# Griffin-style decoder step on one Trainium2 core: the attention scores of a tile's two heads issued alternately

## The chip, the cores and the metric

The kernel runs on one core of a Trainium2 chip. The metric is the device time of one execution in microseconds (us), taken as the median of several runs. Engines are named as in the profile: PE is TensorE's matmul side, PEld its weight loads, DVE is VectorE, ACT is ScalarE, POOL is GpSimd, SP is SyncE (which only issues transfers here).

## The reference, cut to what matters

One layer of a hybrid decoder is applied to a prompt of 1024 tokens and to 8 single new tokens. A recurrent branch (RG-LRU) and an attention branch are merged by gates and followed by a SwiGLU FFN. The change touches the prompt's attention alone. It has three groups of eight heads, each head 64 wide, with (window, dilation) of (128, 1), (512, 4) and (2048, 16). For each head the computation is

```python
s = jnp.einsum('brcqhe,brckhe->brchqk', qb, kb) * (HEAD_DIM ** -0.5)
s = jnp.where(valid[:, None], s + bias, -jnp.inf)
m = jnp.max(s, axis=-1)
p = jnp.exp(s - m[..., None])
l = jnp.sum(p, axis=-1)
o = jnp.einsum('brchqk,brckhe->brcqhe', p, vb.astype(jnp.float32))
```

where a block of 128 queries sees one or two blocks of 128 keys of its own residue class.

## The kernel before, in words

All activations lie transposed, channels on the 128 partitions and the 1032 tokens along the free dimension. Most of the time goes to large projections: weights are split into a high and a low part, and three matmuls of 344 columns per weight tile are summed (line 456, in the function `unit`).

The prompt's attention is a stage of its own (`for g in range(NG)`, line 543 and on for PE). It has three groups g, and for each a loop of four iterations i, twelve iterations in all. One iteration handles one tile of 128 channels, which holds two heads: head 0 on partitions 0 to 63, head 1 on partitions 64 to 127. The tile's queries QT, keys KTT and values VT are loaded by SP, with the bias tables BT of the two heads.

Each iteration has 8 steps, n = 0 to 7. A step is one head hh and one pair of query blocks bp (two blocks of 128 tokens). In the kernel before the order is head, then block pair: `hh, bp = n // 4, n % 4`. A step passes through these operations:

- **scores** on PE, line 576: two matmuls (m = 0, 1) with the head's 64 rows; the result is 128 x 128 or 128 x 256 and goes to the PSUM bank `s_bank[n % 2]`. As data are fp32, each of these matmuls runs as two passes, and each pass is a weight load followed by a MATMUL row in the trace. So a step has four passes of scores.
- scale and bias on DVE (line 1209), row maximum (line 1215), its negative (line 1217); then the exponential on ACT (line 957), in the tile `SB[n % 2]`.
- **turns** on PE, line 587: two to four 128 x 128 transposes of the probabilities with all 128 rows, evacuated by ACT (lines 948 and 950) into `PTS`.
- **values** on PE, line 599: probabilities times values, 128 rows, evacuated by DVE (line 1223).

PE works on three steps at once. Its loop over n runs from 0 to 9, and in turn n it issues the scores of step n, the turns of step n - 1, the values of step n - 2, and then some **pieces** of an unrelated projection (line 556), which keep it busy while DVE and ACT work. The list PIECES sets how many: 7, 5, 4, 4, 4, 4, 3, 3, 3 and 3 pieces of three matmuls in the turns 0 to 9, and 8 pieces stand ahead of turn 0.

```python
PIECES = (8, 15, 20, 24, 28, 32, 36, 39, 42, 45, 48)
...
s_bank = [ups[:, 1, 0, :], ups[:, 1, 1, :]]
pt_bank = [ups[:, 1, 2, :], aux[:, 0, :]]
```

The order is written out by hand and held together by semaphores. For this change these count: `s_mm` (scores of a step are in PSUM, DVE waits for it), `sa_done` (DVE has read a bank of scores, PE waits for it before it writes the bank again, and SP waits for all eight before it loads the next tile), `exp_done` (PE's turns wait for it) and `pt_ev` (values wait for it). For group 0 the tokens of a block lie side by side in QT and KTT; in groups 1 and 2 they are every fourth or every eighth token (the function `toks`), so PE reads them with a stride. The function `nkeys` says how many key blocks a query block sees: in group 0 two, except for the first block; in group 1 alternately one and two; in group 2 one.

Of the kernel before, what the change touches and what calls it, by code (L numbers as in the profile page):

```python
# [28 lines left out]
P = 128  # L29
# [7 lines left out]
HD = 64  # L37
# [55 lines left out]
def build(nc, A, O):  # L93

    with ExitStack() as ctx:
# [174 lines left out]
        def nkeys(g, b):  # L270

            return (2 if b else 1, 1 + b % 2, 1)[g]
# [172 lines left out]
        def _(pe):  # L445
# [100 lines left out]
            for g in range(NG):  # L546
                with pe.Fori(0, 4) as i:
                    def pieces(a, b):
                        for n in range(a, b):
                            slot, c, k = n // 24, n // 8 % 3, n % 8  # L550
                            if n % 24 == 0:
                                pe.wait_ge(w_split[slot], i + (T0[f"att{g}"] + 2))
                            if n % 8 == 0:
                                pe.wait_ge(au_ev, i * 6 + (24 * g + n // 8 + 1))
                            for w, a2 in ((0, 0), (0, 1), (1, 0)):
                                ins = nc.tensor.matmul(ups[:, 0, c, 0:CH], wsp[:, slot, w, k, :], big1[:, a2, k, c * CH:(c + 1) * CH],  # L556
                                                       start=(k == 0 and w + a2 == 0), stop=(k == KT - 1 and w == 1))
                            if n % 8 == 7:
                                ins.then_inc(au_mm if c < NCH - 1 else unit_done[slot], 1)

                    pieces(0, 8)
                    pe.wait_ge(v_ld, i * 16 + 16 * (4 * g + 1))
                    pe.wait_ge(pt_ev, i * 8 + (32 * g + 2))
                    for b in range(8):
                        ins = nc.tensor.transpose(pt_bank[b // 4][:, (b % 4) * P:(b % 4 + 1) * P], toks(VT, g, b), ident[:])
                    ins.then_inc(vt_mm, 1)
                    pe.wait_ge(qk_ld, i * 48 + 48 * (4 * g + 1))
                    for n in range(10):
                        if n < 8:
                            hh, bp = n // 4, n % 4  # L570
                            hr = slice(hh * HD, (hh + 1) * HD)
                            pe.wait_ge(sa_done, i * 8 + (32 * g + n + 1))
                            for m in range(2):
                                b = 2 * bp + m
                                nk = nkeys(g, b)
                                ins = nc.tensor.matmul(s_bank[n % 2][:, 256 * m + 256 - P * nk:256 * m + 256], toks(QT, g, b)[hr],  # L576
                                                       toks(KTT, g, b, nk)[hr], start=True, stop=True)
                            ins.then_inc(s_mm, 1)
                        if 1 <= n <= 8:
                            q = n - 1  # L580
                            pe.wait_ge(exp_done, i * 8 + (32 * g + q + 1))
                            pe.wait_ge(pt_ev, i * 8 + (32 * g + q + 1))
                            if q == 0:
                                pe.wait_ge(vt_ev, i + (4 * g + 1))
                            for m in range(2):
                                for c in range(256 * m + 256 - P * nkeys(g, 2 * (q % 4) + m), 256 * m + 256, P):
                                    ins = nc.tensor.transpose(pt_bank[q % 2][:, c:c + P], SB[q % 2][:, c:c + P], ident[:])  # L587
                            ins.then_inc(pt_mm, 1)
                        if n >= 2:
                            q = n - 2  # L590
                            hh, bp = q // 4, q % 4
                            pe.wait_ge(pt_ev, i * 8 + (32 * g + q + 3))
                            pe.wait_ge(o_ev, i * 8 + (32 * g + q + 1))
                            for m in range(2):
                                b = 2 * bp + m
                                nk = nkeys(g, b)
                                for k in range(nk):
                                    c = 256 * m + 256 - P * (nk - k)
                                    ins = nc.tensor.matmul(o_bank[:, m * (HD + 1):(m + 1) * (HD + 1)], PTS[q % 2][:, c:c + P],  # L599
                                                           VTOK[:, b + 1 - nk + k, hh, :], start=(k == 0), stop=(k == nk - 1))  # L600
                            ins.then_inc(pv_mm, 1)
                        pieces(*PIECES[n:n + 2])
# [132 lines left out]
        def _(act):  # L735
# [149 lines left out]
            for n in range(4):  # L885
                i, j = n // 2, n % 2
# [21 lines left out]
            for g in range(NG):  # L908
                with act.Fori(0, 4) as i:
# [31 lines left out]
                    for n in range(9):  # L941
                        if n >= 1:
                            q = n - 1
                            act.wait_ge(pt_mm, i * 8 + (32 * g + q + 3))
                            act.wait_ge(pv_mm, i * 8 + (32 * g + q + 1))
                            lo = 256 - P * nkeys(g, 2 * (q % 4))
                            if g < 2:
                                ins = nc.scalar.activation(PTS[q % 2][:, lo:512], pt_bank[q % 2][:, lo:512], ACT.Copy)
                            else:
                                ins = nc.scalar.activation(PTS[q % 2].rearrange("p (m c) -> p m c", m=2)[:, :, P:2 * P],  # L950
                                                           pt_bank[q % 2].rearrange("p (m c) -> p m c", m=2)[:, :, P:2 * P], ACT.Copy)
                            ins.then_inc(pt_ev, 1)
                        if n < 8:
                            act.wait_ge(nm_done, i * 8 + (32 * g + n + 1))
                            for m in range(2):
                                cols = slice(256 * m + 256 - P * nkeys(g, 2 * (n % 4) + m), 256 * m + 256)
                                ins = nc.scalar.activation(SB[n % 2][:, cols], SB[n % 2][:, cols], ACT.Exp,  # L957
                                                           bias=NM[:, 2 * (n % 2) + m:2 * (n % 2) + m + 1])
                            ins.then_inc(exp_done, 1)
                        if n in (0, 2, 4, 6, 8):  # L960
                            evac(n // 2)
# [78 lines left out]
        def _(dve):  # L1040
# [154 lines left out]
            for g in range(NG):  # L1195
                per = 2 if g == 1 else 1
                with dve.Fori(0, 4) as i:
# [2 lines left out]
                    step.loop(i, 8)  # L1200
                    for n in range(10):
                        if n < 8:
                            hh, bp = n // 4, n % 4
                            dve.wait_ge(s_mm, i * 8 + (32 * g + n + 1))
                            dve.wait_ge(pt_mm, i * 8 + (32 * g + n + 1))
                            for m in range(2):
                                nk = nkeys(g, 2 * bp + m)
                                cols = slice(256 * m + 256 - P * nk, 256 * m + 256)
                                ins = nc.vector.scalar_tensor_tensor(SB[n % 2][:, cols], s_bank[n % 2][:, cols], SCALE,  # L1209
                                                                     BT[:, hh, 0:P * nk][:, ::-1], ALU.mult, ALU.add)  # L1210
                            ins.then_inc(sa_done, 1)
                            dve.wait_ge(sa_done, i * 8 + (32 * g + n + 3))
                            for m in range(2):
                                cols = slice(256 * m + 256 - P * nkeys(g, 2 * bp + m), 256 * m + 256)
                                ins = nc.vector.tensor_reduce(OT[:, 2 * bp + m, hh, HD + 1:HD + 2], SB[n % 2][:, cols], AX_X, ALU.max)  # L1215
                            step.step(ins)
                            ins = nc.vector.tensor_scalar(NM[:, 2 * (n % 2):2 * (n % 2) + 2], OT[:, 2 * bp:2 * bp + 2, hh, HD + 1],  # L1217
                                                          -1.0, None, ALU.mult).then_inc(nm_done, 1)
                        if n >= 2:
                            q = n - 2  # L1220
                            hh, bp = q // 4, q % 4
                            dve.wait_ge(pv_mm, i * 8 + (32 * g + q + 3))
                            ins = nc.vector.tensor_copy(OT[:, 2 * bp:2 * bp + 2, hh, 0:HD + 1],  # L1223
                                                        o_bank[:, 0:2 * (HD + 1)].rearrange("p (m e) -> p m e", m=2)).then_inc(o_ev, 1)
# [249 lines left out]
```

## Time and profile before

| what | value |
|---|---|
| median of 3 runs | 2247.6 us (2247.16 to 2249.08) |
| profiled execution | span 2250.2 us; no other time is listed for it |
| PE busy | 2160.0 us, 96% of the span |
| PEld busy | 2059.9 us, 92% |
| DVE, ACT, POOL busy | 39%, 23%, 25% |
| share of the final chain on PE | 90% |
| of it line 456, 556, 576 | 62%, 12%, 6% |

Lines 576 (scores), 587 (turns), 599 (values) and 556 (pieces) occur only in the attention stage. A PE row's duration is the time one matmul was under way; neighbours overlap, so what a matmul costs is read from the distance between starts, or from the chain, which gives each piece the time for which it alone held up the end.

### The profile page before, as it was taken

How to read it: one execution, taken by the hardware profiler on the slowest of the kernel's cores; microseconds unless marked ns; L12 is line 12 of the kernel's file. 1: busy time of each engine (PE TensorE's matmuls, PEld its weight loads, DVE VectorE, ACT ScalarE, POOL GpSimd, SP SyncE). 2: the span in 40 equal slices, each digit the busy share in tenths (PEclk: the TensorE clock that was granted, in tenths of full speed). 3: DMA queues.
4: the chain of work that ended last, by engine and by line, in shares of the span. 5: the costliest groups of instructions: out<-in, count | busy, mean ns of one | idle time of the engine just before them, and what ended most of it. 6: DMA issues, size and time to landing. Idle time of an engine off the chain costs nothing.

```text
span 2250.2 us, 33517 instructions
## 1 busy us (share of the span) xinstructions
PE 2160.0 (96%) x13052; PEld 2059.9 (92%) x13052; DVE 877.7 (39%) x1212; ACT 510.9 (23%) x796; POOL 556.6 (25%) x337
## 2 busy tenths in 40 slices
PE   5799899999899999999989999989999999999999
PEld 4799799999888888889989999979999999999999
DVE  8466667777223322232343444261221122211211
ACT  4466533333133332333310001031000000000000
POOL 3232232232311111111111123323333322233322
PEclk9899899999999999999997789989999999999999
DMA  3111022222432233224255334211111111111112
GB/s 123 40 40 48 29 79 75 93 82 86 151 132 89 89 113 117 80 89 139 81 207 222 104 132 149 88 35 47 47 37 47 47 47 47 47 47 47 47 45 87
DMA packets 71402, 188.39 MB, mean 84 GB/s; under 512 B 9257, under 2 KB 28668, under 8 KB 70652
## 3 DMA queue, kind: packets, MB, share of 16 engines
q1 hardware_dynamic: 41392, 136.97, 18.2%
q10 hardware_dynamic: 29964, 50.78, 6.2%
q8 instruction: 31, 0.51, 0.1%
q14 instruction: 15, 0.12, 0.0%
HBM read 145.06 MB, written 45.81 MB: 85 GB/s over the span
## 4 chain that ended last, share of the span: by engine, by line
PE 90%; DVE 5%; issue 1%; ACT 1%; DMA 1%; ACTq 0%; POOL 0%; SPq 0%; DVEq 0%; POOLq 0%
PE ups L456 62%; PE ups L556 12%; PE ups L576 6%; PE aux L599 3%; PE aux L643 1%; PE aux L480 1%; PE aux L621 1%; DVE ext L1066 1%; PE aux L507 1%; PE ups L587 1%; PE aux L587 1%; DVE ext L1062 1%; DVE big L1057 1%; DVE big_f L1051 0%; DVE big L1401 0%
## 5 line engine op out<-in xcount | busy, mean ns | idle before, releaser
L456 PE MATMUL ups<-big,wsp 128*128 128x344 f32 x9360 | 1528.3, 325 | 31.0 <-DVE big L1057 8.2
L456 PEld LDWEIGHTS ups<-big,wsp 128*128 128x128 f32 x9360 | 1501.9, 191 | 54.5 <-issue 26.4
L424 POOL CAST wsp<-wraw 128x1024 fp32r<-128x1024 f32 (+2 forms) x160 | 164.1, 1026 | 1611.6 <-issue 749.6
L426 POOL TENSOR_TENSOR wsp<-wraw,wsp 128x1024 fp32r<-128x1024 f32 (+2 forms) x160 | 380.6, 2379 | 12.8
L556 PE MATMUL ups<-big,wsp 128*128 128x344 f32 x1728 | 304.6, 328 | 6.9 <-ACTq L904 6.9
L556 PEld LDWEIGHTS ups<-big,wsp 128*128 128x128 f32 x1728 | 273.2, 190 | 12.2 <-ACTq L904 7.2
L1162 DVE RECIPROCAL x<-x 128x1024 f32<-128x1024 f32 x24 | 157.3, 6554 | 75.1 <-ACT x L864 75.1
L1209 DVE SCALAR_TENSOR_TENSOR x<-ups,ext 128x128 f32<-128x128 f32 (+1 forms) x192 | 58.7, 348 | 311.9 <-PE ups L576 230.7
L1398 DVE TENSOR_TENSOR ext<-ext,ups 128x1032 f32<-128x1032 f32 x22 | 27.0, 1229 | 373.3 <-PE ups L456 373.3
L576 PE MATMUL ups<-x 64*128 64x128 f32 (+1 forms) x384 | 132.3, 473 | 2.8 <-DMA ext<-bt_s 2.8
L1025 ACT ACTIVATE ext<-ups 128x1032 f32<-128x1032 f32 x22 | 22.7, 1031 | 489.9 <-PE ups L456 489.8
L1410 DVE TENSOR_TENSOR x<-ups,x 128x1032 f32 x24 | 29.6, 1233 | 217.9 <-PE ups L456 217.9
L576 PEld LDWEIGHTS ups<-x 64*128 64x128 f32 x384 | 85.4, 279 | 23.7 <-issue 21.4
L957 ACT ACTIVATE x<-x,ext 128x128 f32<-128x128 f32 (+1 forms) x192 | 76.2, 444 | 82.5 <-DVE ext L1217 82.5
L599 PE MATMUL aux<-ext,x 128*128 128x65 f32 x560 | 73.2, 266 | 0.0
L599 PEld LDWEIGHTS aux<-ext,x 128*128 128x128 f32 x560 | 70.6, 192 | 0.0
L1401 DVE CAST big<-ext 128x1032 f32 x22 | 56.8, 2582 | 7.4 <-DVE ext L1398 7.4
L1215 DVE TENSOR_REDUCE x<-x 128x1 f32<-128x128 f32 (+1 forms) x192 | 57.7, 342 | 3.3
L864 ACT ACTIVATE x<-aux,epst 128x1024 f32<-128x1024 f32 x24 | 26.8, 1117 | 121.2 <-PE aux L507 121.2
L480 PE MATMUL aux<-x,bd 128*128 128x344 f32 x96 | 35.6, 497 | 16.2 <-issue 12.5
L1223 DVE COPY x<-aux 128x130 f32<-128x130 f32 x96 | 27.7, 288 | 44.4 <-PE aux L599 44.4
L1115 DVE SCALAR_TENSOR_TENSOR x<-ext,par,x 128x1024 f32<-128x1024 f32 x24 | 34.1, 1419 | 25.6 <-ACT x L800 23.5
(180 smaller groups left out, 1168.0 us busy)
## 6 DMA issues: line engine op xcount, KB each, us to landing
wraw<-w_in SPq DMA_DIRECT2D x52, 512.0 KB, 3.3
wraw<-w_ffn_in SPq DMA_DIRECT2D x44, 512.0 KB, 3.2
x<-out_qkv SPq DMA_DIRECT2D x36, 512.0 KB, 4.5
out_qkv<-x ACTq DMA_DIRECT2D x32, 512.0 KB, 2.7
x<-gate_s SPq DMA_DIRECT2D x16, 516.0 KB, 4.2
wraw<-w_merge SPq DMA_DIRECT2D x16, 512.0 KB, 5.0
wraw<-w_ffn_out SPq DMA_DIRECT2D x16, 512.0 KB, 3.6
x<-o_s SPq DMA_DIRECT2D x8, 792.0 KB, 6.5
```

What stands on the lines that cost most here:

```text
L424: nc.gpsimd.tensor_copy(hi, raw).then_inc(w_hi, 1)
L426: nc.gpsimd.tensor_tensor(lo, raw, hi.bitcast(F32), ALU.subtract).then_inc(w_split[slot], 1)
L456: ins = nc.tensor.matmul(ups[:, slot, c, 0:CH], wsp[:, slot, w, k, :], src[:, a, k, c * CH:(c + 1) * CH], start=(k == 0 and w + a == 0), s ...
L480: ins = nc.tensor.matmul(aux[:, a, 0:CH], bd[:, a, :], tmp(0)[:, c * CH:(c + 1) * CH], start=True, stop=True)
L556: ins = nc.tensor.matmul(ups[:, 0, c, 0:CH], wsp[:, slot, w, k, :], big1[:, a2, k, c * CH:(c + 1) * CH], start=(k == 0 and w + a2 == 0), s ...
L576: ins = nc.tensor.matmul(s_bank[n % 2][:, 256 * m + 256 - P * nk:256 * m + 256], toks(QT, g, b)[hr], toks(KTT, g, b, nk)[hr], start=True, ...
L599: ins = nc.tensor.matmul(o_bank[:, m * (HD + 1):(m + 1) * (HD + 1)], PTS[q % 2][:, c:c + P], VTOK[:, b + 1 - nk + k, hh, :], start=(k == 0 ...
L957: ins = nc.scalar.activation(SB[n % 2][:, cols], SB[n % 2][:, cols], ACT.Exp, bias=NM[:, 2 * (n % 2) + m:2 * (n % 2) + m + 1])
L1162: step.step(nc.vector.reciprocal(rms_t, rms_t))
L1209: ins = nc.vector.scalar_tensor_tensor(SB[n % 2][:, cols], s_bank[n % 2][:, cols], SCALE, BT[:, hh, 0:P * nk][:, ::-1], ALU.mult, ALU.add)
L1215: ins = nc.vector.tensor_reduce(OT[:, 2 * bp + m, hh, HD + 1:HD + 2], SB[n % 2][:, cols], AX_X, ALU.max)
L1401: step.step(nc.vector.tensor_copy(big2[:, 0, ds(i, 1), :], ext[:, 1, 0:NT]))
```

## The change

The order of the steps becomes block pair, then head: step n is head n % 2 of pair n // 2. PE issues no scores in turns 1, 3, 5 and 7; in turns 0, 2, 4 and 6 it issues those of two steps, n and n + 1, which are the two heads of one block pair. Inside, for each of the two query blocks m, head 0 comes first and head 1 after it, each into its own bank `s_bank[hh]`. The semaphore `s_mm` is raised after the second block of each head. DVE and ACT keep their order of operations; only their indices follow the new order.

```diff
-                        if n < 8:
-                            hh, bp = n // 4, n % 4
-                            hr = slice(hh * HD, (hh + 1) * HD)
-                            pe.wait_ge(sa_done, i * 8 + (32 * g + n + 1))
+                        if n < 8 and n % 2 == 0:
+                            bp = n // 2
+                            pe.wait_ge(sa_done, i * 8 + (32 * g + n + 2))
                             for m in range(2):
                                 b = 2 * bp + m
                                 nk = nkeys(g, b)
-                                ins = nc.tensor.matmul(s_bank[n % 2][:, 256 * m + 256 - P * nk:256 * m + 256], toks(QT, g, b)[hr],
-                                                       toks(KTT, g, b, nk)[hr], start=True, stop=True)
-                            ins.then_inc(s_mm, 1)
+                                for hh in range(2):
+                                    hr = slice(hh * HD, (hh + 1) * HD)
+                                    ins = nc.tensor.matmul(s_bank[hh][:, 256 * m + 256 - P * nk:256 * m + 256], toks(QT, g, b)[hr],
+                                                           toks(KTT, g, b, nk)[hr], start=True, stop=True)
+                                    if m:
+                                        ins.then_inc(s_mm, 1)
...
-                                for c in range(256 * m + 256 - P * nkeys(g, 2 * (q % 4) + m), 256 * m + 256, P):
+                                for c in range(256 * m + 256 - P * nkeys(g, 2 * (q // 2) + m), 256 * m + 256, P):
...
-                            hh, bp = q // 4, q % 4
+                            hh, bp = q % 2, q // 2
```

The same change of indices (`q % 4` to `q // 2`, `n // 4, n % 4` to `n % 2, n // 2`) is made in ACT's evacuation and exponential and in DVE's bias, maximum and copy.

## Rows read from the trace of the kernel before

**Rows 1.** The page's head and its busy time (us, share, instructions).
```profile
span 2250.2 us, 33517 instructions
...
PE 2160.0 (96%) x13052; PEld 2059.9 (92%) x13052; DVE 877.7 (39%) x1212; ACT 510.9 (23%) x796; POOL 556.6 (25%) x337
```

**Rows 2.** Stretch of one iteration, group 0 (busy us of PE, PEld, DVE, ACT, POOL; clock).
```profile
714.00:757.00 43.00, 43.00 (x276) 38.17 (x275) 15.59 (x48) 16.59 (x35) 6.93 (x5) 1.00 0.31 105
```

**Rows 3.** PE's waits (total us, times, longest).
```profile
PE ups L576 <- DMA ext<-bt_s: 2.8, 1, 2.8
```

**Rows 4.** The final chain over the attention stage, 628 to 1142 us, by line.
```profile
by line: PE ups L556 53.9%; PE ups L576 24.5%; PE aux L599 11.2%; PE ups L587 4.3%; PE aux L587 4.2%; PE aux L565 1.0%; PE ups L565 1.0%; issue 0.0%
```

**Rows 5.** The chain in group 0 (start us, us, what, pieces).
```profile
642.05 1.06 PE ups L576 x4
643.11 0.59 PE ups L587 x4
643.70 0.84 PE aux L599 x8
...
646.48 0.85 PE ups L576 x4
```

**Rows 6.** The chain in group 1.
```profile
820.48 1.67 PE ups L576 x4
822.15 0.48 PE aux L587 x3
```

**Rows 7.** The chain in group 2.
```profile
1003.04 1.25 PE ups L576 x4
1004.29 0.37 PE aux L587 x2
```

**Rows 8.** The chain at transposes with no scores ahead of them.
```profile
757.93 0.44 PE aux L565 x4
```

**Rows 9.** PE's timeline, group 0, single passes (start us, us, line, operation, tiles, count).
```profile
641.73 0.32 PE L556 MATMUL ups<-big,wsp 128*128 128x344 f32 x1
641.98 0.48 PE L576 MATMUL ups<-x 64*128 64x256 f32 x1
...
642.30 0.59 PE L576 MATMUL ups<-x 64*128 64x256 f32 x2
...
642.52 0.59 PE L576 MATMUL ups<-x 64*128 64x256 f32 x2
...
643.04 0.33 PE L587 MATMUL ups<-ident,x 128*128 128x128 f32 x1
```

**Rows 10.** The same in group 1.
```profile
820.41 0.60 PE L576 MATMUL ups<-x 64*128 64x128 f32 x1
...
820.83 0.87 PE L576 MATMUL ups<-x 64*128 64x128 f32 x2
...
821.07 1.08 PE L576 MATMUL ups<-x 64*128 64x256 f32 x2
...
821.53 0.63 PE L576 MATMUL ups<-x 64*128 64x256 f32 x1
```

**Rows 11.** The same in group 2.
```profile
1003.40 0.66 PE L576 MATMUL ups<-x 64*128 64x128 f32 x2
...
1003.64 0.65 PE L576 MATMUL ups<-x 64*128 64x128 f32 x2
```

**Rows 12.** Timeline of PE and ACT around step 6, group 0.
```profile
656.00 0.66 PE L587 MATMUL aux<-ident,x 128*128 128x128 f32 x4
...
658.69 1.13 PE L576 MATMUL ups<-x 64*128 64x256 f32 x4
...
657.88 0.91 ACT L957 ACTIVATE x<-x,ext 128x256 f32<-128x256 f32 x2 [0.59 <-DVE ext L1217]
```

**Rows 13.** Timeline of PE and ACT around step 0 of a later iteration, group 0.
```profile
759.15 3.58 PE L556 MATMUL ups<-big,wsp 128*128 128x344 f32 x21
...
762.32 0.80 ACT L957 ACTIVATE x<-x,ext 128x128 f32<-128x128 f32 x2 [1.47 <-DVE ext L1217]
```

More of the change, by code:

```diff
@@ L945, in _ @@
                             act.wait_ge(pv_mm, i * 8 + (32 * g + q + 1))
-                            lo = 256 - P * nkeys(g, 2 * (q % 4))
+                            lo = 256 - P * nkeys(g, 2 * (q // 2))
                             if g < 2:
@@ L955, in _ @@
                             for m in range(2):
-                                cols = slice(256 * m + 256 - P * nkeys(g, 2 * (n % 4) + m), 256 * m + 256)
+                                cols = slice(256 * m + 256 - P * nkeys(g, 2 * (n // 2) + m), 256 * m + 256)
                                 ins = nc.scalar.activation(SB[n % 2][:, cols], SB[n % 2][:, cols], ACT.Exp,
@@ L1202, in _ @@
                         if n < 8:
-                            hh, bp = n // 4, n % 4
+                            hh, bp = n % 2, n // 2
                             dve.wait_ge(s_mm, i * 8 + (32 * g + n + 1))
@@ L1220, in _ @@
                             q = n - 2
-                            hh, bp = q // 4, q % 4
+                            hh, bp = q % 2, q // 2
                             dve.wait_ge(pv_mm, i * 8 + (32 * g + q + 3))
```

## The prediction

> **What bounds the kernel now.** I read first the page's head: PE is busy for 96% of the span [rows 1]. An average hides stages, so next the stretch of one iteration of the attention stage: PE is busy for all of its 43 us, DVE and ACT for little more than a third, with the granted clock at 1.00, the upper of its two levels [rows 2]. The list of PE's waits agrees: ahead of the scores PE waited once, for 2.8 us, on a transfer [rows 3]. So in this stage no engine and no queue holds PE up; each microsecond of PE's own work that goes or comes changes the end by as much, unless it opens a wait. Last, the chain by line tells where PE's time goes: the pieces 53.9%, the scores 24.5% of 514 us, which is 126 us for 96 blocks of scores [rows 4].
>
> What is one block made of? In group 0 it holds the chain for 1.06 us [rows 5]. Its passes start 0.32 us apart at first, then 0.22 us [rows 9]; four passes of 0.216 us make 0.86 us. The remaining **0.195 us is the entry**: the last piece starts 0.25 us ahead of the first pass (0.09 us more than the 0.16 us by which pieces follow each other: 21 take 3.58 us, the last 0.32 us of it alone [rows 9, 13]), and the first weight load is not hidden (0.32 less 0.216 us, 0.10 us). There is **an exit of 0.15 us** too: the four turns behind the scores hold the chain for 0.59 us [rows 5], four transposes with no scores ahead of them for 0.44 us [rows 8]. Entry and exit are where PE goes from instructions on 128 rows to such on 64 and back. In groups 1 and 2 the strided operands make passes slower: 128 columns take 0.235 to 0.24 us, 256 columns 0.46 us [rows 10, 11]. A block of group 1 then has 2 x 0.235 + 2 x 0.46 = 1.39 us of passes in 1.67 us, an entry of 0.28 us [rows 6]; one of group 2 has 0.96 us in 1.25 us, an entry of 0.29 us [rows 7]. Their exits are again 0.15 us (0.48 us for three turns, 0.37 us for two, at 0.11 us a turn) [rows 6, 7, 8].
>
> **The change part by part.**
>
> *Half of the entries and exits go.* Of 96 blocks 48 are left, each of eight passes; those of the odd turns vanish, 16 in each group. Group 0: 16 x (0.195 + 0.15) = 5.5 us; group 1: 16 x 0.43 = 6.9 us; group 2: 16 x 0.44 = 7.0 us. Together **19.4 us** less.
>
> *The order inside a block* becomes, with A for head 0 and B for head 1, A1 A2 B1 B2 A3 A4 B3 B4: three inner changes from one half of the array's rows to the other, 144 in all. No row of this trace has two such halves side by side, so it is bounded from both sides. The cheapest: at each change one pass runs wholly beside another, and eight slots become five (A1, A2 with B1, B2 with A3, A4 with B3, B4). The dearest: a change costs as much as the entry, 0.195, 0.28 or 0.29 us. I take the cheap end, but with weight loads one after the other, since the entry shows that TensorE waits at a change of the kind of instruction (128 rows to 64), and between the heads that kind stays. A load's price: the values, whose 65 columns are short, hold the chain for 0.84 us per eight passes, 0.105 us each, which is the load [rows 5]; for strided weights the entry's unhidden part gives 0.42 less 0.235 us, 0.19 us [rows 10], and I take 0.11 and 0.22 us. A slot with two passes then needs at least two loads.
> - Group 0, 12 pairs with 256 columns throughout: 8 x 0.216 becomes 5 x 0.216, 0.65 us less each, 7.8 us. The 4 pairs that begin with 128 columns: 1.30 us becomes 0.11 + 0.22 + 3 x 0.216 = 0.98 us, 1.3 us in all.
> - Group 1, 16 pairs: 2.78 us becomes 0.235 + 0.44 + 3 x 0.46 = 2.06 us, 11.6 us in all.
> - Group 2, 16 pairs: 8 x 0.24 = 1.92 us becomes 2 x 0.24 + 3 x 0.44 = 1.80 us, 1.9 us in all.
>
> Together **22.6 us** less.
>
> Here a page of the Trainium skill and the trace differ. By row, passes of one half follow at 0.216 us although each has its own load [rows 9], so a load hides under the matmul of the same half. The Trainium skill, "TensorE: Matmul & The Clock Gate", Part 3 (what overlaps and what doesn't), says that a weight load overlaps a running matmul only where the row group differs; by it each of the plain passes would cost 0.32 us, and the 144 changes would hide a load of 0.10 to 0.20 us each, some 24 us in the place of the 22.6 us. The trace excludes the first half of this, and the sum stays with the rows.
>
> *Cover.* A turn of PE waits for the exponential of its step. In the odd turns no scores stand ahead of the turns any more, so the steps of even number lose a block of cover. The tightest is step 6 of group 0: the exponential ended at 658.79 us, 3.10 us after the start of its fourth pass (655.69 us, 0.305 us ahead of the turns at 656.00) [rows 12]. After the change PE has behind that pass the last one of head 1 (0.216 us), the same 0.305 us, and the work from 656.00 to 658.69 less the entry's 0.09 us: 3.12 us. Just covered. Step 0 of group 0 is worse, since ACT gets its input late there, from DVE: in the row shown the exponential ends at 763.12 us [rows 13], while PE would come to its turns at 759.15 + 0.33 (longer block) + 3.41 us = 762.89 us. A wait of 0.3 us; in the other iterations it is about nothing. I charge **0.4 us**. In groups 1 and 2 PE's passes are longer and DVE's work shorter, so the cover is ample. The steps of odd number have their scores a whole turn earlier than before.
>
> *What moves beside it.* DVE, ACT, POOL and their DMAs issue the same operations in the same order. PE's wait on `sa_done` now asks one step more, but for step n - 1, whose scores were issued two turns ago. Behind it on PE are the pieces, and nothing waits for them within a turn. SP's loads of the next tile wait for the last step's bias; its scores come one turn earlier, so they leave earlier by about what the iteration gets shorter. All this at nothing; if that cover failed, the price would be a wait like the 2.8 us of [rows 3] in some of 12 iterations.
>
> The sum: 19.4 + 22.6 - 0.4 = 41.6 us less. Against the profiled execution's 2250.2 us [rows 1] that is 2208.6 us; this execution lies 2.6 us above the median of the runs, 2247.6 us, so on their scale **2206 us**.
>
> **The rivals.**
>
> *Loads overlap too.* If the two halves also load side by side, all five slots are as long as one pass: 9.5 us in group 0, 14.9 in group 1, 11.5 in group 2, 35.9 us. With 19.4 us and waits of 0.6 us it is 54.7 us, **2193 us**. For it: a load and a matmul of one half run beside each other already [rows 9]. Against it: loads of one half stand in line [rows 5], and no row has another half. The Trainium skill, "TensorEngine Tiling (Array Packing)", Tiling Modes, states that different tiles can load weights and multiply in parallel, which is this case.
>
> *No overlap at all.* The passes stay in line, the change of half is free, and only entries and exits are saved: 19.4 us, **2228 us**. The change then would not do what the alternation suggests. For it: the two heads share the columns of the array and the moving side, and all pass rates in the rows are those of a single stream. Against it: operands, banks and rows of the two are apart.
>
> *A change of half is an entry* (the slower side). Its place is inside the block, between A2 and B1, B2 and A3, A4 and B3. If TensorE empties itself and loads unhidden there, it costs 3 x 16 x (0.195 + 0.28 + 0.29) = 36.7 us, less 19.4 us: 17.3 us more, **2265 us**. It decides from 19.4 / 144 = 0.135 us per change on. For it: entry and exit show that TensorE can pay at a change of rows. Against it: those are changes of size as well.
>
> *A part of an entry.* Only the emptying (0.09 us) gives 13.0 - 19.4, 2241 us; only the unhidden load (0.10, 0.19, 0.20 us) gives 23.8 - 19.4, 2252 us.
>
> **How the numbers follow.** Forecast 0.38; loads overlap too 0.17; no overlap 0.18; a part of an entry 0.11; a whole entry 0.16. A measurement of this kernel tells changes of over 0.2%, 4.5 us, from none. Faster takes the first three and 0.03 of the fourth: 0.76. The same: 0.05 of the fourth. Slower: the last 0.03 of it and the fifth, 0.19. The range goes from 2189 us (the second case with its waits and load prices better than counted) to 2252 us (the partial entry's upper end) and leaves out the whole entry. The first three cases, which hold most of the chance, reach from 2189 to 2231 us by themselves.
>
> **What would show it.** In the chain of the changed kernel, the eight passes of a block: about 1.08 us in group 0, 2.06 in group 1 and 1.80 in group 2, plus an entry as before, if the forecast holds; 0.87 to 1.08, 1.85 and 1.2 with parallel loads; 1.73, 2.78 and 1.92 without overlap; more than 2.2 us in group 0 with entries inside. In the timeline A2 and B1 start together or they don't, and the pieces of odd turns are followed by turns at 0.16 us with no entry. PE's waits should stay as they are, but for a few tenths on ACT ahead of the turns of step 0. It is wrong if waits of PE on ACT or DVE grow to tens of us in the stage, or if lines 456 and 556 change their times.

## The result, and the profile after

The changed kernel takes 2177.9 us (median of 4 runs, 2176.4 to 2183.6) where the kernel before took 2248.3 us beside it. The ratio is 0.969, with a 95% interval of 0.9675 to 0.9704: 70.4 us less. In a later set of runs it was 0.9685 (0.9667 to 0.9703). It is faster, as forecast, but by far more than the 41.6 us of the prediction, and the time lies below the range.

The page's head of the changed kernel, with its costliest lines of the chain:

```profile
span 2174.6 us, 33529 instructions
...
PE 2081.3 (96%) x13052; PEld 2011.1 (92%) x13052; DVE 870.1 (40%) x1212; ACT 505.9 (23%) x796; POOL 555.4 (26%) x337
...
PE ups L456 65%; PE ups L556 12%; PE ups L577 3%; PE aux L601 3%; PE aux L645 1%; PE aux L480 1%; PE aux L623 1%; DVE ext L1068 1%; PE aux L507 1%; PE aux L589 1%; DMA o_s<-x 1%; PE ups L589 1%; DVE ext L1064 1%; DVE big L1059 1%; DVE big_f L1053 0%
```

PE's share of the span is what it was [rows 1]: the same number of instructions, in less time. The scores (now line 577) went from 6% of the chain to 3%. The chain inside the stage shows why, in groups 0, 1 and 2 (start us, us, what, pieces; line 589 are the turns, line 601 the values):

```profile
641.33 1.06 PE ups L577 x8
642.39 0.59 PE aux L589 x4
...
797.09 1.68 PE ups L577 x8
798.77 0.48 PE aux L589 x3
...
951.50 1.25 PE ups L577 x8
952.75 0.37 PE aux L589 x2
```

These are the numbers of [rows 5 to 7], but with eight passes in the place of four: a block of two heads costs what a block of one head cost, entry and exit included. On PE the second head's scores are free.

Stretches of one iteration each, first of the kernel before (groups 0, 1, 2), then of the changed one (us of the stretch; busy us of PE, PEld, DVE, ACT, POOL; granted clock):

```profile
714.00:756.90 42.90, 42.90 (x276) 38.07 (x275) 15.59 (x48) 16.59 (x35) 6.83 (x5) 1.00 0.31 104
891.80:938.10 46.30, 46.30 (x258) 39.28 (x257) 13.50 (x48) 14.16 (x32) 6.85 (x5) 1.00 0.29 97
1025.00:1065.10 40.10, 40.10 (x234) 36.66 (x233) 12.08 (x48) 12.44 (x32) 6.81 (x5) 1.00 0.33 112
```

```profile
702.85:741.30 38.45, 38.45 (x276) 35.74 (x276) 15.23 (x48) 16.25 (x35) 6.84 (x5) 1.00 0.34 116
858.10:897.10 39.00, 39.00 (x257) 35.42 (x256) 13.00 (x48) 13.70 (x32) 6.81 (x5) 1.00 0.35 115
1006.10:1040.70 34.60, 34.60 (x234) 32.69 (x233) 10.86 (x48) 11.98 (x32) 6.80 (x5) 1.00 0.40 129
```

An iteration lost 4.5, 7.3 and 5.5 us. It has four blocks of scores where it had eight. The four that are gone, of 1.15 us on average in group 0, 1.82 in group 1 and 1.40 in group 2, with entry and exit, would be 4.6, 7.3 and 5.6 us. Twelve iterations make 69 us, which is the whole result within the runs' spread. PE is busy for all of each of these stretches, so it still bounds the stage. PE's waits in the whole stage:

```profile
PE ups L577 <- DMA ext<-bt_s: 1.3, 1, 1.3
PE ups L589 <- ACT x L959: 1.2, 3, 0.7
```

The wait on ACT ahead of the turns of step 0 is of the kind that the prediction named, 1.2 us where 0.4 was charged. Two of the three, 0.3 and 0.2 us, lie in group 0, where the prediction put them; the longest, 0.7 us, lies in group 2, whose cover it called ample. The chain leads from that one back to the store of the tile before, which DVE waits for:

```profile
968.93 6.45 DMA o_s<-x
...
975.77 0.29 DVE x L1211
...
977.12 0.39 ACT x L959
...
977.63 0.43 PE ups L589 x2
```

How can two heads take the time of one? PE's timeline over 0.3 us of a block in group 0, at its start:

```profile
641.01 0.32 PE L556 MATMUL ups<-big,wsp 128*128 128x344 f32 x1
641.26 0.49 PE L577 MATMUL ups<-x 64*128 64x256 f32 x2
```

Two passes together take 0.49 us where one alone took 0.48 us [rows 9], so they start within 0.01 us of each other. Passes of one half never start so close in the kernel before (0.32 and 0.22 us apart), so these must be the first pass of head 0 and the first of head 1. The same holds for the loads, two of which take 0.19 us where one alone takes 0.18 us. Here are those of the first 0.1 us:

```profile
641.26 0.19 PEld L577 LDWEIGHTS ups<-x 64*128 64x128 f32 x2 [0.21 <-issue]
```

### The profile page after: what moved, and what is told of

Same layout as the page of the kernel before. It is cut to its first block, busy times and chain, and to the rows that moved or that the text cites. A ratio compares the mean times of both kernels' runs of the same rounds, so it can differ in the third digit from the quotient of the medians.

```text
span 2174.6 us, 33529 instructions
## 1 busy us (share of the span) xinstructions
PE 2081.3 (96%) x13052; PEld 2011.1 (92%) x13052; DVE 870.1 (40%) x1212; ACT 505.9 (23%) x796; POOL 555.4 (26%) x337
## 4 chain that ended last, share of the span: by engine, by line
PE 90%; DVE 5%; DMA 2%; issue 1%; ACT 1%; ACTq 0%; POOL 0%; DVEq 0%; SPq 0%; POOLq 0%
PE ups L456 65%; PE ups L556 12%; PE ups L577 3%; PE aux L601 3%; PE aux L645 1%; PE aux L480 1%; PE aux L623 1%; DVE ext L1068 1%; PE aux L507 1%; PE aux L589 1%; DMA o_s<-x 1%; PE ups L589 1%; DVE ext L1064 1%; DVE big L1059 1%; DVE big_f L1053 0%
## 5 line engine op out<-in xcount | busy, mean ns | idle before, releaser
L577 PE MATMUL ups<-x 64*128 64x128 f32 (+1 forms) x384 | 66.5, 473 | 1.3 <-DMA ext<-bt_s 1.3
L577 PEld LDWEIGHTS ups<-x 64*128 64x128 f32 x384 | 43.1, 278 | 11.1 <-issue 8.1
```

The lines of the kernel that those rows point to most:

```text
L577: ins = nc.tensor.matmul(s_bank[hh][:, 256 * m + 256 - P * nk:256 * m + 256], toks(QT, g, b)[hr], toks(KTT, g, b, nk)[hr], start=True, sto ...
```

## The experiments

There are seven runs in two sets, each set on one chip and beside the kernel before.

**Two steps of one head in a block.** This has the blocks of the changed kernel (48 of them, eight passes each), but all passes lie on one half of the rows.

```diff
+                        if n < 8 and n % 2 == 0:
+                            hh = n // 4
...
+                            for m in range(2):
+                                for s in range(2):
+                                    b = 2 * ((n + s) % 4) + m
...
+                                    ins = nc.tensor.matmul(s_bank[s][:, 256 * m + 256 - P * nk:256 * m + 256], toks(QT, g, b)[hr],
+                                                           toks(KTT, g, b, nk)[hr], start=True, stop=True)
```

> The old order of steps (head, then block pair), but PE issues the scores of steps n and n + 1 together in the even turns, as the changed kernel does. The two steps belong to one head, so all eight passes lie on the same half of the array's rows, and 48 of 96 blocks are left. Theory (the two halves run side by side, and only different halves do): passes stay in line, and only the entries and exits are saved, 19.4 us; about 2229 us, eight passes of group 0 taking some 1.73 us. Rival (the overlap comes from two banks or from issuing two steps at once, whichever the half): as fast as the changed kernel, about 2178 us.

It took 2250.3 us, a ratio of 1.0008 (0.9994 to 1.0022): no gain that can be told, so both theories missed, the first by 21 us and the rival by 72. The passes did stay in line. But where are the 19.4 us? The chain of this kernel in group 0 and in group 2:

```profile
719.67 1.92 PE ups L577 x8
721.59 0.59 PE aux L589 x4
...
1034.47 2.20 PE ups L577 x8
1036.67 0.37 PE aux L589 x2
```

Eight passes in line and one entry: 8 x 0.216 + 0.195 = 1.92 us, and 8 x 0.24 + 0.29 = 2.21 us. The turns behind them take what they took [rows 5, 7]. Per block, entry and exit are saved as worked out. Now one iteration each of groups 0, 1 and 2:

```profile
710.20:751.60 41.40, 41.40 (x276) 38.58 (x275) 14.69 (x48) 16.03 (x35) 6.80 (x5) 1.00 0.31 108
...
887.60:936.60 49.00, 49.00 (x258) 44.28 (x257) 13.29 (x48) 13.37 (x32) 6.85 (x5) 0.90 0.27 91
...
1024.70:1063.10 38.40, 38.40 (x234) 36.68 (x233) 11.15 (x48) 12.00 (x32) 6.89 (x5) 1.00 0.35 117
```

Groups 0 and 2 gained 1.5 and 1.7 us per iteration (four entries and exits are 1.4 and 1.8 us). Group 1 lost 2.7 us, and there the granted clock is 0.90: a mean of 0.90 means that for a fifth of the stretch, 9.8 us, it was at 1.2 GHz, the lower of its two levels. That costs an estimated 4.9 us, and without it the iteration would be 44.1 us, 2.2 us shorter than before (four entries and exits are 1.7 us). What PE did before the clock fell: blocks of eight passes on one half, strided, 3.05 us long, where before a block took 1.67 us:

```profile
851.64 3.05 PE ups L577 x8
854.69 0.83 PE aux L589 x3
```

The turns behind that block took 0.83 us, not 0.48 [rows 6]: they ran at the lower clock (granted clock 0.50 from 854.2 to 861.0 us). The saving was lost in group 1, as the stretches of groups 1 and 2 as a whole show:

```profile
785.00:980.00 195.00, 195.00 (x1042) 176.15 (x1041) 53.47 (x193) 54.53 (x131) 27.44 (x16) 0.91 0.29 98
980.00:1138.00 158.00, 158.00 (x941) 151.03 (x939) 44.63 (x192) 47.97 (x128) 27.40 (x16) 0.98 0.29 99
```

By the same estimate the lower level cost 17.5 us in group 1 and 3.2 us in group 2, together about what entries and exits saved. It was so in every execution: the mean granted clock of this kernel is 0.957 to 0.963 in all ten, that of the kernel before 0.968 to 0.976 in the nineteen beside them.

**The same rows for both heads.** The changed kernel, but for one line:

```diff
-                                    hr = slice(hh * HD, (hh + 1) * HD)
+                                    hr = slice(0, HD)
```

> The changed kernel, but the matmuls of head 1 read the rows of head 0 (partitions 0 to 63); the scores of head 1 are left out, all else stays, order and banks too. Theory (only different halves overlap): the eight passes stand in line, 50.6 us more than the changed kernel, about 2229 us, the same as with two steps of one head in a block. Rival (order and banks make the overlap): no difference, about 2178 us.

It took 2251.0 us, a ratio of 1.0012 (0.9998 to 1.0026). Order and banks are those of the changed kernel, and the whole gain is gone; the operands' partitions alone make it. But 2251.0 us is 73 us more than the changed kernel, not the 50.6 us that were expected. The passes are in line, as in the first experiment, and the clock has the same marks, 0.90 in group 1. First the chain of a block in group 0, then the stretches of the three groups:

```profile
675.46 1.92 PE ups L577 x8
...
623.00:786.00 163.00, 161.87 (x1072) 150.52 (x1071) 58.86 (x191) 63.85 (x138) 23.95 (x14) 1.00 0.32 111
786.00:980.00 194.00, 194.00 (x1022) 175.15 (x1021) 53.17 (x192) 53.55 (x129) 27.39 (x16) 0.90 0.27 93
980.00:1138.00 158.00, 158.00 (x939) 151.04 (x939) 45.18 (x194) 47.92 (x128) 27.34 (x16) 0.98 0.29 99
```

At 0.90 and 0.98 the lower level costs an estimated 19.4 us in group 1 and 3.2 us in group 2; with 50.6 us for the passes that is 73.2 us.

**One head after the other, inside the block.** The changed kernel with its two inner loops exchanged, so that the program has both matmuls of head 0 and then both of head 1.

```diff
-                            for m in range(2):
-                                b = 2 * bp + m
-                                nk = nkeys(g, b)
-                                for hh in range(2):
-                                    hr = slice(hh * HD, (hh + 1) * HD)
+                            for hh in range(2):
+                                hr = slice(hh * HD, (hh + 1) * HD)
+                                for m in range(2):
+                                    b = 2 * bp + m
+                                    nk = nkeys(g, b)
```

> The changed kernel, but inside a block both matmuls of head 0 come first and then both of head 1, in place of alternating by query block. Theory A (matmuls start in the order of the program, each with its two passes, and a half only looks at the next one): head 1 begins beside the second matmul of head 0, six slots in place of four where columns are equal, 21 us more than the changed kernel, about 2199 us. Theory B (each half has its own queue that runs ahead of the other's): no difference, about 2178 us. Theory C (only neighbours that are issued directly behind one another overlap, pass by pass): one slot in eight saved, 2215 to 2228 us.

It took 2177.6 us, a ratio of 0.968 (0.966 to 0.9705), the changed kernel's time. Theory B holds: the alternation that gives the change its name is not needed. The first block of an iteration of group 0 shows it by its shapes, since each head has one matmul of 128 columns and then one of 256. The passes that PE ran in the first 0.3 us of that block, by shape:

```profile
L577 PE MATMUL ups<-x 64*128 64x128 f32 x4 | 0.5, 323 | 0.0
L565 PE MATMUL aux<-ident,x 128*128 128x128 f32 x1 | 0.3, 273 | 0.0
```

All four passes of 128 columns, of both heads, stand ahead of any pass of 256, though in the program head 0's 256 columns come before head 1's 128. So the second half overtakes the first. The Trainium skill, "TensorE: Matmul & The Clock Gate", Part 3 (what overlaps and what doesn't), has matmuls start and end strictly in program order; across two halves the starts of this run show otherwise.

**Two steps of one head, in group 0 only**, to see whether the clock was what ate the saving:

```diff
+                        if g == 0 and n < 8 and n % 2 == 0:
...
+                        if g and n < 8:
```

> The kernel before, with the scores of two steps of one head issued together in group 0 only; groups 1 and 2 stay as they were. Theory (the entries and exits are a real price, and in the kernel with all three groups paired this way their saving was eaten by stretches at half clock, which lie in groups 1 and 2): no half clock in the stage and 16 x 0.345 = 5.5 us less, about 2243 us. Rival (the saving is lost in waits or elsewhere, whatever the clock): no change, 2248 us.

It took 2242.5 us, a ratio of 0.997 (0.9956 to 0.9984): 6.5 us less than the 2249.0 us beside it, with 5.5 worked out; by the interval it is 3.6 to 9.9 us. Its stretch of group 1, with blocks as in the kernel before:

```profile
786.00:972.00 186.00, 186.00 (x1033) 157.94 (x1032) 54.31 (x193) 56.79 (x129) 27.39 (x16) 1.00 0.28 96
```

The clock is 1.00. With long one-half blocks in group 1 it was 0.90, without them it is not: the price of entry and exit is real, and with the sums of the first experiment the clock was what hid it there.

**The changed kernel again** was run beside the last three.

> The changed kernel once more, beside the next three on one chip. Every theory expects its time again, about 2178 us, a ratio of 0.969.

2179.4 us, as told at the top. In its profile PE waited on ACT not once in the stage, so the 1.2 us seen above come and go.

**A later wait for the store.** The changed kernel, with DVE's wait on `o_stored` moved.

```diff
-                    dve.wait_ge(o_stored, i * (16 * per) + 16 * stores)
...
                             dve.wait_ge(sa_done, i * 8 + (32 * g + n + 3))
+                            if n == 0:
+                                dve.wait_ge(o_stored, i * (16 * per) + 16 * stores)
```

> The changed kernel, with DVE's wait for the store of the previous tile moved from ahead of the bias of step 0 to ahead of its row maximum, the first write to the stored tile. Theory (the waits of PE ahead of the turns of step 0 are DVE's lateness behind that store, 0.76 us at most of which is the bias in group 0): PE's waits on ACT in the stage vanish but for one, and the time falls by 1 to 2 us, to some 2176 us. Rival (something else is late next, and PE waits for that): no change, 2178 us.

2179.7 us, a ratio of 0.9686 (0.9668 to 0.9703): no difference from the changed kernel can be told, and the 1 to 2 us that the theory expected do not show. DVE's wait for the store did go, from 80.9 us in the changed kernel's stage (56.5 us in its second profile) to 2.7 us in this one's:

```profile
DVE x L1211 <- DMA o_s<-x: 80.9, 10, 9.2
```

```profile
DVE x L1218 <- DMA o_s<-x: 2.7, 6, 0.5
```

PE never waited on ACT here, but neither did it in the changed kernel's second profile, so this run does not tell whether the store causes such waits. Idle time of 50 to 80 us on an engine that doesn't bound the stage was worth nothing that can be measured.

**Four steps in a block in group 2**, on top of the later wait. A step of group 2 fills half of a bank, so two block pairs fit.

```diff
+                        per_block = 4 if g == 2 else 2
+                        if n < 8 and n % per_block == 0:
...
+                                    at = 256 * m + 256 - P * nk - (P if g == 2 and bp % 2 else 0)
...
+                            dve.wait_ge(s_mm, i * 8 + (32 * g + (n // 4 * 4 + 4 if g == 2 else n + 1)))
```

> As the one before, and in group 2, where a step fills only half of a bank, the scores of four steps (two block pairs, both heads) are issued in one block, and DVE waits for all four. Theory (each entry and exit costs 0.44 us in group 2, whatever the number of passes behind it): 8 blocks fewer, 3.5 us less than the kernel with the later wait alone, some 2173 us. Rival (a longer block costs the clock, as with one half, or uncovers the exponential): no gain, or a loss.

2176.6 us, a ratio of 0.9669 (0.9653 to 0.9686). The median is 3.1 us under that of the kernel without the fours, with 3.5 expected, but the intervals overlap, so a gain in the total isn't shown. In the trace it is there: an iteration of group 2 takes 33.6 us, against 34.6 us, and the longer blocks left the clock at 1.00.

```profile
971.00:1004.60 33.60, 33.60 (x233) 32.71 (x233) 10.91 (x48) 11.78 (x32) 6.76 (x5) 1.00 0.40 133
```

## Why the prediction was right or wrong

**What bounds the stage** was right: but for 2.5 us of waits PE is busy through the whole stage after the change too, and its saved time came out at the end one for one.

**Entries and exits** (19.4 us) were right in size. One-half blocks gave 1.5 and 1.7 us per iteration in groups 0 and 2, and 6.5 us in the run with group 0 alone; two blocks fewer per iteration of group 2 gave 1.0 us in the last run, with 0.9 worked out. In the changed kernel itself they aren't seen apart from the rest. The step missed that a longer block can cost the clock. In the changed kernel it cost nothing: there a block is no longer than before, and the clock stayed at 1.00.

**The step that failed** is "eight slots become five", with "weight loads one after the other": 22.6 us. It took the passes of both heads as one line in the order of the program, so that head 1 could begin beside head 0's second pass at the earliest. The runs showed two lines in place of one. The starts 0.01 us apart, the equal time with the heads in turn and the order of passes there say that each half takes its own matmuls, loads its own weights and does not wait for the other, so that eight passes take four slots, of the length of four passes of one head. By the prediction's own pass times that is half of 101 us, 50.6 us (25.9 in group 0, 44.5 in group 1, 30.7 in group 2, halved), and with 19.4 us it is 70.0 us, against 70.4 measured. The term was mis-sized by 28 us.

The rival with parallel loads was nearer (54.7 us) and had the loads right, but it carried the five slots too, and so did the low end of the range: the bound called "the cheapest" was not the cheapest. A head that is wholly hidden behind the other would have been the true bound. The Trainium skill, "TensorEngine Tiling (Array Packing)", Tiling Modes, which that rival cites, agrees with the trace in both of its points, loads and matmuls in parallel (both start within 0.01 us); its overview's factor of up to two for 64 rows is what the passes show, eight in the 1.06 us of four.

**No overlap**, **a change of half is an entry** and **a part of an entry** fell: starts 0.01 us apart leave no room for any of them. **Cover** was right for group 0 and missed group 2; it is small (1.2 us in one profile, none in another). **What moves beside it** cost nothing beyond these waits.

## What to carry to other kernels

Where a matmul contracts over 64 rows, look for a second one on the other 64 and issue it next to the first, into another bank: here it was free, loads too, and the order of the two in the program made no difference. When bounding an overlap that no row shows, take as the cheap end that the second stream vanishes, not what a guess at the queue allows. And where passes are gathered into longer blocks, read the granted clock of each stretch before crediting a saving.

## What the runs showed of the hardware that was not expected

- The two halves of the rows worked as two streams for these fp32 matmuls. Passes started 0.01 us apart in the changed kernel, and with one head's matmuls all ahead of the other's in the program the second half still overtook the first.
- Entry and exit are paid once for both halves: a block of eight passes side by side in group 0 takes the 1.06 us of four, 0.195 us of entry included, and the turns behind it the same 0.59 us.
- The clock fell to its lower level in group 1 when eight strided passes of one half stood in line (3.05 us a block), in two kernels, and stayed at 1.00 with eight passes on two halves (1.68 us) or four on one (1.67 us). With the long one-half blocks of group 2 (2.20 us) it was 0.98. What exactly makes it fall was not pursued. Nor was it tried to let both halves write one bank.
